# Matrix memory of a streaming encoder layer: mask and row values as one-pass products, one denominator link less

## The reference, cut to what matters

```python
b = jnp.cumsum(lf, axis=-1)
dmat = jnp.where(causal, b[..., :, None] - b[..., None, :] + ig[..., None, :], -jnp.inf)
inter = b + m[..., None]
m_t = jnp.maximum(inter, jnp.max(dmat, axis=-1))
s_inter = jnp.exp(inter - m_t)
wqk = jnp.exp(dmat - m_t[..., None]) * jnp.einsum('bhtd,bhsd->bhts', q, k)
num = s_inter[..., None] * jnp.einsum('bhtd,bhde->bhte', q, c) + jnp.einsum('bhts,bhse->bhte', wqk, v)
den = s_inter * jnp.einsum('bhtd,bhd->bht', q, n) + jnp.sum(wqk, axis=-1)
h = num / jnp.maximum(jnp.abs(den), jnp.exp(-m_t))[..., None]
```

## Time and profile before

| What | Value |
|---|---|
| median of 3 runs | 2739.98 us (2737.26 to 2744.63) |
| profiled execution: span | 2986.5 us (the page gives no other time of it) |
| instructions | 40647 |
| PE busy | 2816.7 us, 94% |
| DVE busy | 1558.9 us, 52% |
| ACT busy | 1353.2 us, 45% |
| POOL busy | 606.0 us, 20% |
| mean granted TensorE clock | 0.796 of full speed |

### The profile page before, as it was taken

One profiled execution on the slowest core, in us unless ns is written; L12 is line 12 of the kernel. 1 busy time (PEld: TensorE's weight loads), 2 busy tenths in 40 slices (PEclk: granted clock), 3 DMA queues, 4 the chain that ended last, 5 costly groups with the idle time before them and its releaser, 6 DMA issues. The chain is left out here.

```text
span 2986.5 us, 40647 instructions
## 1 busy us (share of the span) xinstructions
PE 2816.7 (94%) x15116; PEld 2432.3 (81%) x15116; DVE 1558.9 (52%) x2505; ACT 1353.2 (45%) x2119; POOL 606.0 (20%) x492
## 2 busy tenths in 40 slices
PE   8999999999998899999998989799999999999991
PEld 7888786777766799999996747589998989999991
DVE  4555232113645644444443347476767676666774
ACT  4555321103532533333332132267767776676762
POOL 1000100002301101011011302333333334333333
PEclk7777777777776688888888878788888888888885
DMA  8211222203087155454444231488888888888864
GB/s 240 61 49 48 67 64 97 89 29 113 1 282 222 35 134 154 127 143 128 117 124 145 74 108 64 133 254 244 269 251 254 266 241 271 241 269 249 259 201 151
DMA packets 389358, 467.97 MB, mean 157 GB/s; under 512 B 17469, under 2 KB 312533, under 8 KB 389242
## 3 DMA queue, kind: packets, MB, share of 16 engines
q1 hardware_dynamic: 367144, 395.81, 42.8%
q0 software_dynamic: 17760, 60.34, 8.4%
q10 hardware_dynamic: 4338, 10.23, 0.9%
HBM read 397.62 MB, written 68.70 MB: 156 GB/s over the span
## 5 line engine op out<-in xcount | busy, mean ns | idle before, releaser
L3327 PE MATMUL banks<-slot_rowsT,expert_w_high 128*128 128x384 f32 x2048 | 611.9, 367 | 0.0
L3329 PE MATMUL banks<-slot_rowsT,expert_w_low 128*128 128x192 f32 x2048 | 527.9, 258 | 0.0
L3329 PEld LDWEIGHTS banks<-slot_rowsT,expert_w_low 128*128 128x128 f32 x2048 | 404.8, 198 | 1.6
L3327 PEld LDWEIGHTS banks<-slot_rowsT,expert_w_high 128*128 128x128 f32 x2048 | 391.0, 191 | 2.7 <-issue 0.4
L3367 ACT CAST expert_w_high<-expert_w 128x2048 fp32r<-128x2048 f32 x128 | 237.6, 1905 | 19.2 <-DMA expert_w<-in_exp_w 19.2
L3426 DVE TENSOR_TENSOR expert_w_low<-expert_w,expert_w_high 128x2048 fp32r<-128x2048 f32 x96 | 216.7, 2284 | 30.5 <-ACT expert_w_high L3367 30.5
L2208 PE MATMUL banks<-xT_chunk_high,w_gates_high 128*128 128x384 f32 x576 | 204.1, 354 | 4.5 <-DVE xT_chunk_low L2280 4.5
L2209 PE MATMUL banks<-xT_chunk_low,w_gates_high 128*128 128x384 f32 x576 | 207.9, 361 | 0.0
L3252 POOL TENSOR_TENSOR expert_w_low<-expert_w,expert_w_high 128x2048 fp32r<-128x2048 f32 x32 | 147.1, 4596 | 287.0 <-ACT expert_w_high L3367 287.0
L2210 PE MATMUL banks<-xT_chunk_high,w_gates_low 128*128 128x384 f32 x576 | 204.9, 356 | 0.0
L3467 DVE TENSOR_TENSOR expert_w_low<-expert_w,expert_w_high 128x1024 fp32r<-128x1024 f32 x128 | 156.7, 1224 | 56.4 <-ACT expert_w_high L3396 56.4
(11 more groups left out here) (510 smaller groups left out, 6583.1 us busy)
## 6 DMA issues: line engine op xcount, KB each, us to landing
expert_w<-in_exp_w SPq DMA_DIRECT2D x126, 1024.0 KB, 8.5
expert_w<-in_exp_w SPq DMA_DIRECT2D x32, 2048.0 KB, 10.5
w_gates<-in_w_in SPq DMA_DIRECT2D x72, 512.0 KB, 4.5
cached_k<-in_cache_sb_k SPq DMA_DIRECT2D x16, 1024.0 KB, 9.2
cached_v<-in_cache_sb_v SPq DMA_DIRECT2D x16, 1024.0 KB, 9.8
w_stream<-in_w_in SPq DMA_DIRECT2D x48, 256.0 KB, 4.2
w_proj<-in_w_pa SPq DMA_DIRECT2D x24, 512.0 KB, 5.2
w_stream<-in_w_in SPq DMA_DIRECT2D x16, 512.0 KB, 5.5
```

The costliest lines, as they stand in the source:

```text
L3327: nc.tensor.matmul(out[:, 0:2 * SLOTS], hi, xgT[:, par, k].rearrange("p a s -> p (a s)"), start=(k == 0), stop=(k == DT - 1), skip_group_c ...
L3329: last = nc.tensor.matmul(out[:, 0:SLOTS], lo, xgT[:, par, k, 0, :], start=False, stop=(k == DT - 1), skip_group_check=True)
```

## The change

Two things change in `stage_mlstm`. The mask product takes the identity and the masks as float32r, a form that PE runs in one pass. The row values are split into three rounded float32r parts (high part, rounded rest, and what is left), which lie at partitions 0, 32 and 64 of a [96, 1152] tile whose other rows are zero; a selector with ones at the three places sums them in one one-pass product per head. In `divide` the two instructions for the absolute value become one.

The parts, the selector and the rounded masks are made in `stage_sb_prompt`, in the first steps of its engine lists. They stay in memory on the right side until `stage_mlstm` ends.

```diff
@@ stage_sb_prompt
+        rest = ctx.enter_context(nc.sbuf_tensor("ml_w_row_rest", [H, T], F32R))
 @block.scalar
             for s in range(N + LAG):
+                if s == 1:
+                    act.wait_ge(parts_zeroed, 2)
+                    nc.scalar.copy(m.w_parts[0:H], m.w[:]).then_inc(parts_high, 1)
+                if s == 2:
+                    act.wait_ge(parts_left, 1)
+                    nc.scalar.copy(m.w_parts[32:32 + H], m.w[:])
+                    nc.scalar.copy(rest[:], m.w[:]).then_inc(parts_high, 1)
+                    for n, tile in enumerate((g.ident, g.causal, g.causal_s)):
+                        nc.scalar.copy(m.masks[:, n, :], tile[:])
                 if s >= LAG:
                     move_w(s - LAG)
 @block.gpsimd
+            pool.memset(m.w_parts[:].bitcast(F32), 0.0).then_inc(parts_zeroed, 1)
+            pool.memset(m.sel_parts[:].bitcast(F32), 0.0).then_inc(parts_zeroed, 1)
+            pool.wait_ge(parts_zeroed, 2)
+            for part in range(3):
+                rows = m.sel_parts[32 * part:32 * part + 32]
+                pool.affine_select(out=rows, in_=rows.bitcast(F32), compare_op=ALU.not_equal, fill=1.0,
+                                   base=0, pattern=[[-1, H], [0, P]], channel_multiplier=1).then_inc(parts_zeroed, 1)
+                pool.wait_ge(parts_zeroed, 3 + part)
 @block.vector
                 if 1 <= s <= N:
                     scan(s - 1)
+                if s == 1:
+                    dve.wait_ge(parts_high, 1)
+                    nc.vector.tensor_tensor(m.w[:], m.w[:], m.w_parts[0:H].bitcast(F32), ALU.subtract
+                                            ).then_inc(parts_left, 1)
+                if s == 2:
+                    dve.wait_ge(parts_high, 2)
+                    dve.wait_ge(parts_left, 1)
+                    nc.vector.tensor_tensor(m.w_parts[64:64 + H], m.w[:], rest[:].bitcast(F32), ALU.subtract)
@@ stage_mlstm, scores
-                nc.tensor.matmul(g.bank[0][:], g.ident[:], mask[:].unsqueeze(1).broadcast_to([P, H, P]), start=True,
+                nc.tensor.matmul(g.bank[0][:], m.masks[:, 0, :],
+                                 m.masks[:, 2 if i == NT - 1 else 1, :].unsqueeze(1).broadcast_to([P, H, P]), start=True,
                                  stop=False, skip_group_check=True)
                 for h in range(H):
-                    last = nc.tensor.matmul(g.bank[0][:, h * P:(h + 1) * P], g.sel[:, h, :], m.w[:, cols],
+                    last = nc.tensor.matmul(g.bank[0][:, h * P:(h + 1) * P], m.sel_parts[:, h, :], m.w_parts[:, cols],
@@ stage_mlstm, divide
-                link(nc.vector.tensor_scalar(den[:, 0], num[:, :, HD], -1.0, None, ALU.mult))
-                link(nc.vector.tensor_tensor(den[:, 1], den[:, 0], num[:, :, HD], ALU.max))
+                link(nc.vector.scalar_tensor_tensor(out=den[:, 1], in0=num[:, :, HD], scalar=-1.0, in1=num[:, :, HD],
+                                                    op0=ALU.mult, op1=ALU.max))
@@ build_program
+                    m.w_parts, m.sel_parts = (
+                        parts.enter_context(nc.sbuf_tensor(name, shape, F32R, side="right"))
+                        for name, shape in (("ml_w_row_parts", [96, T]), ("head_selector_parts", [96, H, P])))
+                    m.masks = parts.enter_context(nc.sbuf_tensor("ident_and_masks", [P, 3, P], F32R, side="right"))
```

More of the change, by code:

```diff
@@ L1213, in load_ahead, with stage_sb_prompt @@
             self.load_v(sp, v)
-def stage_sb_prompt(nc, g, qT, kT, v_tok, cache):
+def stage_sb_prompt(nc, g, qT, kT, v_tok, cache, m):
     units = [(h, qb) for h in range(H) for qb in (4, 3, 5, 2, 6, 1, 7, 0)]
@@ L1238, in stage_sb_prompt @@
         y_moved = sem("p_y_moved")
+        rest = ctx.enter_context(nc.sbuf_tensor("ml_w_row_rest", [H, T], F32R))
+        parts_zeroed = sem("p_parts_zeroed")
+        parts_high = sem("p_parts_high")
+        parts_left = sem("p_parts_left")
         block = ctx.enter_context(nc.Block())
@@ L1830, in scores @@
                 cols = slice(i * P, (i + 1) * P)
-                mask = g.causal_s if i == NT - 1 else g.causal
                 if i:
                     pe.wait_ge(dexp_ready, i)
-                nc.tensor.matmul(g.bank[0][:], g.ident[:], mask[:].unsqueeze(1).broadcast_to([P, H, P]), start=True,
+                nc.tensor.matmul(g.bank[0][:], m.masks[:, 0, :],
+                                 m.masks[:, 2 if i == NT - 1 else 1, :].unsqueeze(1).broadcast_to([P, H, P]), start=True,
                                  stop=False, skip_group_check=True)
                 for h in range(H):
-                    last = nc.tensor.matmul(g.bank[0][:, h * P:(h + 1) * P], g.sel[:, h, :], m.w[:, cols],
+                    last = nc.tensor.matmul(g.bank[0][:, h * P:(h + 1) * P], m.sel_parts[:, h, :], m.w_parts[:, cols],
                                             start=False, stop=(h == H - 1), skip_group_check=True)
@@ L3648, in build_program @@
                         stage_sb_project(nc, g, x_hi, x_lo, qT, kT, v_tok, k_new, v_new, stream)
+                    parts = early.enter_context(ExitStack())
+                    m.w_parts, m.sel_parts = (
+                        parts.enter_context(nc.sbuf_tensor(name, shape, F32R, side="right"))
+                        for name, shape in (("ml_w_row_parts", [96, T]), ("head_selector_parts", [96, H, P])))
+                    m.masks = parts.enter_context(nc.sbuf_tensor("ident_and_masks", [P, 3, P], F32R, side="right"))
                     cache = CacheRing(nc, early.enter_context(ExitStack()), g)
-                    stage_sb_prompt(nc, g, qT, kT, v_tok, cache)
+                    stage_sb_prompt(nc, g, qT, kT, v_tok, cache, m)
                     prompt.close()
@@ L3663, in build_program @@
                     stage_mlstm(nc, g, m, ycT, mix_early.load_ahead)
+                parts.close()
                 xT = early.enter_context(nc.sbuf_tensor("xT", [P, DT, T], F32, side="right"))
```

## The result

| Kernel | Median | Ratio to before, 95% interval |
|---|---|---|
| before | 2739.81 us (13 runs) | |
| changed | 2745.2 us (13 runs, 2742.16 to 2749.8) | 1.0018 (1.001 to 1.0026) |

By the ratio the change costs 4.9 us (the two medians are 5.4 us apart). The forecast was 2736 us and no change that can be told. The time lies within the range of 2728 to 2746 us, but the direction is wrong, and clearly so: the interval of the ratio lies above one.

What follows compares the result with a forecast made beforehand. PE was taken to bound both stages. Tiles -12.7, stall +6.0 and clock +1.2 gave -5.5 us at the profile's clock, -1.3 at a faster one; -4 was taken: 2736 us, range 2728 to 2746 (8 in 10).

Steps and rivals of the forecast that it cites:

- The gain in the tiles: Matrix memory: eight tiles, each 1.65 us shorter, win 12.7 us at the profile's clock, 8.3 at the runs'.
- The one-pass products: Matrix memory tile: mask and row products take 0.85 us instead of 2.56, PE's tile 5.48 instead of 7.19.
- What is late next: Matrix memory tile: DVE comes next as the limit, with a floor of 5.45 us beside PE's 5.48.
- The link: Division in the matrix memory: dropping one instruction brings nothing by itself, but lowers DVE's floor by about 0.2 us.
- The stall: Start of the attention on the prompt: the preparation makes PE's first product by the values 6.0 us late.
- The clock: Attention, behind PE's gap of some 4.7 us: the granted clock falls and costs 1.2 us.
- That the stall isn't won back: Attention on the prompt: the 6.0 us stay lost, because PE bounds the stage (busy 58.4 of 60 us).
- The second: Rival, matrix memory: DVE takes over or products keep their pace; 4 to 5 us won, 7 lost, 2742 us; 22 in 100.
- The third: Rival, attention: PE's clock stays near 0.5 after the stall; 2750 us; 5 in 100.
- The signs: Changed kernel's profile: tile about 5.5 us, PE gap 4 to 5 us in the attention, clock near 0.5 behind it.

Runs made afterwards that it cites:

- b0: The kernel before, unchanged, traced once more at a clock of 0.966, that of the runs; its span is 2740.4 us.
- e2: The kernel before with only the denominator link dropped (two instructions for the absolute value become one); ratio 1.0012.
- e7: The kernel before with the BN_AGGR of the prompt tiles moved to the end of the matrix memory stage; ratio 1.0004.
- e9: The kernel before with the one-pass mask product and shorter division, its three mask copies made in the attention on the samples; row products unchanged; ratio 0.9994.
- e5: The changed kernel with the whole preparation moved to the attention on the samples; ratio 0.9988 to the kernel before.
- e6: The changed kernel with the preparation in the attention on the samples and the prompt tiles' BN_AGGR at the stage's end; ratio 0.9983 to before.
- e4: The kernel before plus the preparation alone at the start of the attention on the prompt, row values kept in their own tile; ratio 1.004.
- e8: The changed kernel with four useless products on PE ahead of the first product by the values; ratio 1.0007 to the kernel before.
- e3: The changed kernel with the preparation spread over steps 9 to 18 of the attention on the prompt; ratio 1.0005 to the kernel before.
- e1: The changed kernel with the products and division of before, preparation alone; row values overwritten, so later work differs; ratio 1.0055 to before.
- e10: The kernel before with one-pass mask product, shorter division, mask copies on the samples, and BN_AGGR at the stage's end; ratio 0.9988.

## Why the prediction was wrong, point by point

- **The gain in the tiles: the step that failed.** The sum took 12.7 us for it at the profile's clock and 8.3 at the runs', and put the truth in between; 5.7 us were measured, under both. The profiled execution had a clock of 0.75 in the tiles; b0 has 1.00. A tile of before is 5.71 us there, not 7.19 and not the 6.6 that I made by scaling it with the ratio of the time to the span (0.917). That ratio is a mean over stretches that go with the clock and stretches that don't; the tile shrank to 0.79 of its time. By the clock alone it would be 5.39 us; e2 and e7 show that DVE isn't what holds it at 5.71, and what the other 0.3 us are stays open. DVE's floor doesn't go with the clock (5.45 us forecast, 5.37 measured), so less was left to win: 0.34 us from 5.71 to 5.37 in the later tiles, more only in the first ones.
- **The one-pass products: right, even cautious.** 0.71 us stand for 2.04 in a tile where PE doesn't wait, and PE's tile fell from 5.71 to 4.26 us. The row product of 96 rows comes every 0.1 us. But e9 shows that behind the first tile the mask alone would have brought the same.
- **What is late next: right.** DVE's floor was forecast at 5.45 us and is 5.37 (e5, the changed kernel), and e6 moves it. What I missed is that the floor doesn't hold from the first tile: the second and third take 4.26 and 4.69 us, a slack of DVE that the quick PE uses up there. Without that the gain would have been smaller still.
- **The link: right.** e2 shows no gain in the tiles.
- **The stall: right in mechanism, and in size partly by luck.** 6.0 us forecast, 6.0 measured at PE's first product by the values; 5.2 by DVE's third scan. ACT's wait is 3.63 us, PE's gap 4.74. But the terms differ: DVE's first multiplication ends 1.1 us later than in b0, not 0.4, because GpSimd's masks come later, and unit 2's sigmoids start 6.8 us later, not 6.0. What made up for it is ACT's own wait of 0.67 us for PE's turned weights, which stands ahead of the move in b0 and is gone in the changed kernel.
- **The clock: a cost that was there, but size off and cause not shown.** 1.2 us forecast. The attention lost 8.5 us in all, so 2.5 beside the stall. At a full clock the lower level costs half of the time and not a third: I had priced it from 0.75, and some 5 us of PE's work ran at 0.50. The next burst started at half the clock, as the rule of the Trainium skill that was weighed there has it ("TensorE: Matmul & The Clock Gate", "HAM oscillation — how this bites in real kernels"). But in the trace the long gap isn't what brought the clock down: it was at 0.50 when the gap began, behind a wait of 2.67 us, in e4 it fell within the first us of the gap, and in e8 although PE had no gap there. b0 has 1.53 us in place of the 2.67, and no fall. Which idle time brought the fall wasn't tested.
- **That the stall isn't won back: right**, and e3 shows it in the main for copies placed later as well. I had read the attention as bound by PE; at the full clock PE is busy 8.65 and DVE 8.16 us of 10, and PE waits 8.6 us in 13 places for ACT's moves (b0). That a chain over all four engines binds the stage is how I read this; no experiment made one of its links shorter.
- **Between the stages: not forecast.** 3.1 us lie between the attention on the prompt and the tiles. The changed kernel's trace has the clock at 0.87, 0.50 and 0.78 in the first three windows of 2 us of the samples' stage, and once more lower (0.85) 82 us into it; e1 has the same. The first of these dips cost 1.4 us: the first product by the keys starts 5.5 us into the stage in both, 4.1 in b0. e7, e8 and e10 have such a dip 54 us into it, and take 1.8 to 2.1 us more than b0. b0, e2, e3, e4 and e9 have no dip in the first 84 us and take 93.8 to 94.4 us. e4 has the preparation of the changed kernel, and e7 has none and ran the program of before up to there, with the same share of busy time on PE at the place of the dip (1.02 and 2.00 of 2 us). So the extra time goes with the dips, and that the change brings them isn't shown. Without the 3.1 us the stretches add up to 2.4 us more than before, a little under the interval of the runs (2.7 to 7.1 us). What makes the clock dip in one execution and not in another, and in how many of the timed executions it did, stays open.
- **The rivals.** The second (DVE takes over at the runs' clock, a third of the gain, 2742 us) is the one that came true; I gave it 22 in 100. Its sum, 5 won and 7 lost, is near what was measured, 5.7 and 8.5. The third (the clock doesn't come back) is refuted: it is at 1.00 from 616 on.
- **The signs.** The main ones came true: a tile of about 5.5 us, a gap of 4 to 5 us, a clock near 0.5 behind it. They look at the kernel after only. The tile of before at the runs' clock, against which 5.5 us is little gain, wasn't among them.

The remedy follows from it: the gain stays when the preparation goes where ACT and DVE have time (e5, e6). Three copies and one line in `scores` (e9, with the link) bring all of it behind the first tile, without any splitting into parts; in the whole time e9's gain can't be told, and with the BN_AGGR moved (e10) it is 0.9988 (0.9978 to 0.9999).

## What to carry to other kernels

Compare the profiled execution with the runs before a sum is made: here it was 9% longer, at a clock of 0.796 against 0.966, and so the gain on PE was taken too large and the price of the lower clock too small. Scale a stretch by its own clock and not by the ratio of the spans (a tile went to 0.79 of its time here, the clocks to 0.75, the spans to 0.92), and leave the other engines' time as it is. Work that is off the critical engine isn't free where a pipeline fills or where the other engines' lists are links of PE's loop: put it in a stage in which they wait. And when an engine gets a shorter tile, ask how many tiles there are: eight may be over before the next engine's floor is felt, as in e9.

## What the runs showed of the hardware

- A float32r product with 96 rows and 128 columns follows the one before it after 0.1 us, its fresh weights included (four in 0.39 us, clock 1.00); the float32 product that it replaces takes 0.27.
- Behind a gap of 4.74 us PE ran at half the clock for some 5 us (0.58 in the window from 607 to 617), but the clock had been at 0.50 from the start of the gap, behind a wait of 2.67 us. With useless products in place of the gap it fell as well (0.53, 0.52) and was back at 1.00 before the needed products began (e8).
- The same program with the same work has a dip of the clock to 0.50 in one execution (e7 at 752.80 to 754.80) and none in another (b0 at 755.50 to 757.50), worth some 2 us in the stretch.
- Whole executions of one program begin the attention 597.0 to 604.7 us into the span, while the attention on the prompt behind it repeats to 0.1 us where the clock is the same (97.2 to 97.3 us in seven traces).
